# Two-bank query head, joined column units and one moved remainder in a two-block fp32 transformer kernel

## What is computed

```python
def second_block(x, norm1_g, w_in, ..., normf_g):
    h = x
    xn = rmsnorm_2(h, norm1_g)
    q_a, k_a, v_a, q_r, f_r, i_r, g_r = split(xn @ w_in)       # 7 x 512 columns
    attn = moba_attention(q_a, k_a, v_a)
    rec  = hgrn2(q_r, f_r, i_r, g_r, lb, rec_norm_g)           # f = lb + (1-lb)*sigmoid(f_r); silu(q_r); log f; cumsum
    h = h + concat([attn, rec]) @ w_out
    hn = rmsnorm_2(h, norm2_g)
    h = h + peer_2(hn, peer_wq, peer_subkeys, peer_u, peer_v)
    return rmsnorm_2(h, normf_g)

def peer_2(...):                                               # the first block has the same stage
    qp = (xb @ wq).reshape(T, HEADS, 2, 128)                   # 8 heads, two halves: 16 tiles of 128 columns
    s  = einsum('thcd,hcnd->thcn', qp, subkeys)                # 128 scores per head and half, top 16 of each
    ...                                                        # softmax over 16 experts, gelu(x u), times v
```

## Time and profile before

| | |
|---|---|
| median of 3 runs | 1984.23 us (1984.2 to 1984.7) |
| profiled execution | 1984.3 us, span 1982.5 us |
| TensorE matmul busy | 1974.8 us (100%), 13990 matmuls |
| VectorE busy | 1281.9 us (65%) |
| ScalarE busy | 1042.3 us (53%) |
| GpSimd busy | 1429.7 us (72%) |
| DMA | 177 GB/s over the span, 53.2% of 16 engines' span |

### The profile page before, as it was taken

The page is one execution under the profiler, slowest core; times in us unless marked ns, Lnnn a source line. Parts: engine busy times, 40 slices in busy tenths (PEclk is TensorE's granted clock), DMA queues, the critical chain, the costliest instruction groups (busy, mean ns, idle before and its releaser), DMA issues.

```text
span 1982.5 us, 39083 instructions
## 1 busy us (share of the span) xinstructions
PE 1974.8 (100%) x13990; PEld 1766.6 (89%) x13990; DVE 1281.9 (65%) x2178; ACT 1042.3 (53%) x1361; POOL 1429.7 (72%) x606
## 2 busy tenths in 40 slices
PE   9999999999999999999999999999999999999998
PEld 9899898888888888888889899888888888888887
DVE  5256387864766899953336738886467789994333
ACT  6556545565555544445447665556555554444444
POOL 6667878888777878854448757888877787884442
PEclk9999999999999999999999999999999999999999
DMA  8444545555555555566655345555555555555653
GB/s 273 161 139 149 179 161 186 188 183 190 177 170 175 174 169 171 177 208 206 195 186 178 123 144 166 192 187 186 182 176 172 172 178 169 175 174 181 201 190 127
DMA packets 100467, 351.44 MB, mean 177 GB/s; under 512 B 12464, under 2 KB 15408, under 8 KB 100272
## 3 DMA queue, kind: packets, MB, share of 16 engines
q1 hardware_dynamic: 99680, 348.61, 53.2%
q10 hardware_dynamic: 720, 1.92, 0.3%
HBM read 349.44 MB, written 1.05 MB: 177 GB/s over the span
## 4 chain that ended last, share of the span: by engine, by line
PE 99%; DMA 0%; DVE 0%; ACT 0%; POOL 0%; SPq 0%; issue 0%
PE ps L1259 24%; PE ps L1325 12%; PE ps L1260 12%; PE ps L1327 12%; PE ps L1328 6%; PE ps L1326 6%; PE ps L732 4%; PE ps L734 4%; PE ps L733 4%; PE ps L889 4%; PE ps L1251 3%; PE ps L891 2%; PE ps L816 1%; PE ps L1235 1%; PE ps L1137 1%; PE ps L926 1%
## 5 line engine op out<-in xcount | busy, mean ns | idle before, releaser
L653 POOL TENSOR_TENSOR wlo<-ring,whi 128x1024 fp32r<-128x1024 f32 x567 | 1375.2, 2431 | 511.3 <-ACT whi L1677 425.8
L1677 ACT ACTIVATE whi<-ring 128x1024 fp32r<-128x1024 f32 x536 | 566.5, 1060 | 718.2 <-PE ps L1328 387.2
L1259 PE MATMUL ps<-hboth,whi 128*128 128x512 f32 x2048 | 714.6, 395 | 0.0
L1260 PE MATMUL ps<-hboth,wlo 128*128 128x256 f32 x2048 | 567.7, 277 | 0.0
L1259 PEld LDWEIGHTS ps<-hboth,whi 128*128 128x128 f32 x2048 | 384.1, 188 | 87.2
L1325 PE MATMUL ps<-whi,shi 128*128 128x512 f32 x1024 | 404.2, 395 | 0.0
L1327 PE MATMUL ps<-wlo,shi 128*128 128x512 f32 x1024 | 400.4, 391 | 0.0
L1260 PEld LDWEIGHTS ps<-hboth,wlo 128*128 128x128 f32 x2048 | 384.7, 188 | 0.0
L1328 PE MATMUL ps<-whi,slo 128*128 128x256 f32 x1024 | 286.7, 280 | 0.0
L1326 PE MATMUL ps<-whi,slo 128*128 128x256 f32 x1024 | 285.7, 279 | 0.0
L1327 PEld LDWEIGHTS ps<-wlo,shi 128*128 128x128 f32 x1024 | 192.2, 188 | 43.4
(11 more groups left out here) (332 smaller groups left out, 2905.2 us busy)
## 6 DMA issues: line engine op xcount, KB each, us to landing
ring<-in_weights SPq DMA_DIRECT2D x651, 512.0 KB, 3.3
act<-in_const SPq DMA_DIRECT2D x11, 198.0 KB, 4.0
act<-in_const SPq DMA_DIRECT2D x8, 192.0 KB, 4.5
xres<-in_x SPq DMA_DIRECT2D x4, 256.0 KB, 4.9
act<-in_keys ACTq DMA_DIRECT2D x1, 1024.0 KB, 4.7
ring<-in_weights SPq DMA_DIRECT2D x2, 256.0 KB, 4.8
act<-in_fgain ACTq DMA_DIRECT2D x1, 512.0 KB, 3.4
out<-act SPq DMA_DIRECT2D x1, 512.0 KB, 2.6
```

Source lines behind the costliest of these rows:

```text
L653: pool.tensor_tensor(wlo[:, j, :], ring[:, j, :], whi[:, j, :].bitcast(F32), ALU.subtract)\
L1259: pe.matmul(bank(b), whi[:, j, c], hboth[:, :, kc, :], start=kc == 0, stop=False, skip_group_check=True)
L1260: mm = pe.matmul(bank(b, 0, S), wlo[:, j, c], hhi[:, kc, :], start=False, stop=kc == KC - 1, skip_group_check=True)
L1677: eng.activation(whi[:, j, :], ring[:, j, :], ACT.Copy).then_inc(hi_ready[j], 1)
```

## The change

Four edits are made. Units 1, 2 and 3 of the second attention go through `joined_columns()` with banks 6/7, 4/5 and 6/7; ScalarE copies the high-by-low half out of both banks to `col_part`, VectorE adds it back into the banks, and then makes the multiplication by R from there. With it the high copies of ScalarE move: one is now made ahead of the copy, one ahead of the logarithm. For the last query head of each expert stage, tile 0 goes to bank 5 and tile 1 to bank 4, each is copied by itself, and TensorE waits for the copy of head 6 before tile 1. The remainder of the third query slot of each stage goes from GpSimd to VectorE, behind the second square.

```diff
+JOINED2_BANK = {1: 6, 2: 4, 3: 6}
...
+        col_part = carve(cat_at, 2, S)[0]
...
-                lows(at, first, range(RING))
+                query = FIRST[f"q{b}"] // RING
+                lows(at, query, range(RING))
+                lows(query, query + 1, (0, 1, 3))
+                lows(query + 1, first, range(RING))
...
+                        elif i in JOINED2_BANK:
+                            joined_columns(FIRST["in2"] + HALVES * i, JOINED2_BANK[i], None if i == 1 else [(col_copied, i - 1)] * TT)
...
+                            if h + c == HEADS:
+                                pe.wait_ge(n["q_copied"], h)
+                            dst = bank(5 - c, 0, S) if h == HEADS - 1 else bank(4 + h % 2, c * S, (c + 1) * S)
+                            tile((2 * h + c) % RING, dst, R, range(4 if h + c == 1 else 0, KC))
...
+                            if i in JOINED2_BANK:
+                                highs_to(FIRST["in2"] + HALVES * i + 1 + RING)
+                                eng.wait_ge(slot_used, FIRST["in2"] + HALVES * (i + 1))
+                                if i > 1:
+                                    eng.wait_ge(col_joined, i - 1)
+                                b = JOINED2_BANK[i]
+                                eng.activation(col_part, ps[:, b:b + 2, S:2 * S], ACT.Copy).then_inc(col_parted, 1)
...
                     elif what == "rec_prep":
+                        highs_to(FIRST["in2"] + HALVES * 2 + 1 + RING)
                         eng.wait_ge(fr_bound, REC_H)
...
+                            for c in range(2):
+                                eng.wait_ge(slot_used, first_q + 2 * h + c + 1)
+                                last = eng.activation(qT[:, h % 2, c, :], bank(5 - c, 0, S), ACT.Copy)
+                            last.then_inc(n["q_copied"], 1)
...
                 square(k, 1)
+                eng.wait_ge(hi_ready[2], FIRST[f"q{i + 1}"] // RING + 1)
+                eng.tensor_tensor(wlo[:, 2, :], ring[:, 2, :], whi[:, 2, :].bitcast(F32), ALU.subtract).then_inc(lo_ready[2], 1)
                 raw_low(k, 2, rlo, rhi)
...
+                        if i in JOINED2_BANK:
+                            b = JOINED2_BANK[i]
+                            product = ps[:, b:b + 2, 0:S]
+                            eng.wait_ge(col_parted, i)
+                            eng.tensor_tensor(product, product, col_part, ALU.add).then_inc(col_joined, 1)
+                            eng.wait_ge(col_joined, i)
+                        else:
+                            product = bank(4 + i % 2).rearrange("p (j t) -> p j t", j=2)
+                            eng.wait_ge(slot_used, FIRST["in2"] + HALVES * (i + 1))
+                        eng.tensor_tensor(colT[name][:, off // P:off // P + 2, :], product, R, ALU.mult).then_inc(col_copied, 1)
```

More of the change, by code:

```diff
@@ L445, in block_program @@
         col_copied = sem("columns_copied")
+        col_parted = sem("columns_low_part_copied")
+        col_joined = sem("columns_parts_joined")
         fr_open = sem("forget_opened")
@@ L918, in joined_columns @@
                     for t in range(TT):
-                        if half == 0:
+                        if half == 0 and free is not None:
                             pe.wait_ge(*free[t])
@@ L1221, in experts @@
                                 pe.wait_ge(n["q_copied"], h - 1)
-                            tile((2 * h + c) % RING, bank(4 + h % 2, c * S, (c + 1) * S), R, range(4 if h + c == 1 else 0, KC))
+                            if h + c == HEADS:
+                                pe.wait_ge(n["q_copied"], h)
+                            dst = bank(5 - c, 0, S) if h == HEADS - 1 else bank(4 + h % 2, c * S, (c + 1) * S)
+                            tile((2 * h + c) % RING, dst, R, range(4 if h + c == 1 else 0, KC))
                             if h + c == 1:
@@ L1446, in highs_to @@
                     eng.activation(whi[:, m % RING, :], ring[:, m % RING, :], ACT.Copy).then_inc(hi_ready[m % RING], 1)
-                split[0] = end
+                split[0] = max(split[0], end)
             def turned(k):
@@ L1685, in experts @@
                     if h < HEADS:
-                        eng.wait_ge(slot_used, first_q + 2 * h + 2)
+                        if h < HEADS - 1:
+                            eng.wait_ge(slot_used, first_q + 2 * h + 2)
                         if h >= 2:
                             eng.wait_ge(n["s_ready"], h - 1)
-                        eng.activation(qT[:, h % 2, :, :], bank(4 + h % 2).rearrange("p (c t) -> p c t", c=2), ACT.Copy)\
-                           .then_inc(n["q_copied"], 1)
+                        if h < HEADS - 1:
+                            eng.activation(qT[:, h % 2, :, :], bank(4 + h % 2).rearrange("p (c t) -> p c t", c=2), ACT.Copy)\
+                               .then_inc(n["q_copied"], 1)
+                        else:
[3 more added lines that the diff above has]
+                            last.then_inc(n["q_copied"], 1)
                         for c in range(2):
@@ L2164, in attention2 @@
                             take_scale(2)
-                        eng.wait_ge(slot_used, FIRST["in2"] + HALVES * (i + 1))
-                        eng.tensor_tensor(colT[name][:, off // P:off // P + 2, :],
-                                          bank(4 + i % 2).rearrange("p (j t) -> p j t", j=2), R, ALU.mult).then_inc(col_copied, 1)
+                        if i in JOINED2_BANK:
[4 more added lines that the diff above has]
+                            eng.wait_ge(col_joined, i)
+                        else:
+                            product = bank(4 + i % 2).rearrange("p (j t) -> p j t", j=2)
+                            eng.wait_ge(slot_used, FIRST["in2"] + HALVES * (i + 1))
+                        eng.tensor_tensor(colT[name][:, off // P:off // P + 2, :], product, R, ALU.mult).then_inc(col_copied, 1)
                     elif what == "m_values":
```

## The result

The changed kernel takes 1988.47 us (median of 16 runs, 1988.04 to 1989.32) against 1984.45 for the kernel before (1983.86 to 1985.89): the ratio is 1.0020, with a 95% interval of 1.0013 to 1.0027. It is 4.0 us slower, where 1.05 us of gain were forecast and 1985.4 was the upper end of the range. The profiled execution took 1988.04 us, with a span of 1986.2.

What follows compares the result with a forecast made beforehand. TensorE was taken to bound the kernel, with matmuls covering 1974.8 of 1982.5 us. Savings of 0.33 + 0.58 + 0.14 - 0 = 1.05 us off 1984.3 gave 1983.2 us, with a range of 1982.4 to 1985.4.

Steps and rivals of the forecast that it cites:

- the part on the last query head: End of each stage's queries: an earlier last copy removes TensorE's 0.07 us of standing, 0.14 us in two blocks, at no cost.
- The sum: Whole kernel: 0.33 + 0.58 + 0.14 - 0 = 1.05 us off the profiled execution's 1984.3 us, giving 1983.2 us.
- the cadence among the rivals: Expert stage: changed arrival flips 1024 pairs from 0.346 to 0.353 us, costing 7 us, near 1990; chance 0.02.
- The joined units: Units 1 to 3 of the second attention: 5.65 in place of 5.76 us each, 0.33 us saved for three.
- the other cadence: Joined units of the second attention run at 0.346 us a pair: 0.66 us saved in all, 1982.9 us; chance 0.11.
- the nearest row: Joined units: the first attention's cadence, 0.353 us a pair, was taken because pairs there also directly follow matmuls of 256 columns.
- The moved remainder: Third query tile of each stage: subtraction on VectorE ends TensorE's standing and slow restart, 0.30 + 0.28 = 0.58 us saved.
- What gets later: VectorE in the second attention: running sum 2.3 to 3.0 us late, 0.1 after level 2's factor, no cost to TensorE.
- The running sum: VectorE in the second attention: once shifted, it finds GpSimd at the end of a remainder, after lasting 4.35 us before.
- The slack: Turn of the second attention's first probabilities: 0.80 us before, 0.47 us when TensorE is 0.33 us early.
- the late chain: Second attention: delayed levels make TensorE wait at the first turn; 2.3 us late costs 1.8 us, 1985.0 us; chance 0.22.

Runs made afterwards that it cites:

- the single edit: The kernel before with the last query head's edit alone (two banks, two copies): 1989.64 us against 1984.26, ratio 1.0026.
- the kernels with 16 and with 17 fillers: The changed kernel with its 16 short matmuls (29 ns each) on iota ahead of each expert stage's first pair, and with 17: 1988.47 and 1983.10 us.
- 17, 1 and 18 fillers: The changed kernel with 17, 1 or 18 in place of 16 short matmuls ahead of each stage's first pair: 1983.10, 1982.00 and 1983.19 us.
- 0, 15 and 16: The changed kernel with 0 or 15 short matmuls ahead of each stage's first pair, and with its own 16: 1987.43, 1992.33 and 1988.47 us.
- the one whose copies both wait: The changed kernel, but ScalarE waits for both tiles of the last query head ahead of the first copy: 1983.40 us, ratio 0.9998.
- the kernel before with 14: The kernel before with 14 in place of 16 short matmuls ahead of each stage's first pair: 1984.18 us, ratio 1.0001.

## Why the prediction was wrong

The step that failed is in the part on the last query head: "the 0.07 us goes, in two blocks 0.14 us ... Cost: nothing". The mechanism was as told and the 0.07 us did go, twice. But that standing lay eight scores and 16 short matmuls (1.4 us) ahead of a row of 416 equal pairs, and with it taken away and nothing else changed the row ran in the slower of its two cadences. The sum had no term for a cost outside the edited place. The cost is 5.5 us (the single edit, its gain counted in: +5.4 in the medians), some forty times the gain.

I had the cadence among the rivals, with a chance of 0.02, and put it at near 1990. What I set against it was wrong: "both stages start behind the same instructions as before". They do, and it is no argument: the kernels with 16 and with 17 fillers start behind the same instructions too. My own had the same form at 353 and at 346 ns a pair in one kernel; that should have told me that the cadence isn't fixed by the instruction, and that an edit ahead of such a row can put the whole row at stake, here 2.75 us a stage. As for size, I took one stage of 1024 pairs at 7 ns; it was two stages with 416 each at 6.6. That 1990 came near 1988.47 is in part luck: the two errors, in the number of stages and of pairs, work against each other.

The other steps, one by one:

- The joined units. Forecast 0.33 us, with 0.66 in the other cadence; measured 0.64. From 1052.97 to 1069.69 are 16.72 us, of which 0.08 is the start behind the transposes, for 48 pairs: 346.7 ns each. The choice of the nearest row ("pairs follow directly on matmuls of 256 columns") failed: the first unit follows on the two transposes of the token scale. Whether that is why they ran fast isn't shown; one short matmul ahead of the units of the first attention left those slow. The Trainium skill (TensorE: Matmul & The Clock Gate, section Back-to-back issue gap) gives a formula for the gap of a single warm matmul, by which a pair takes an estimated 325 ns. The rows here have two values, 346.7 and 353.3, and neither is that.
- The moved remainder. Forecast 0.30 and 0.28, measured 0.29 and 0.28. The subtraction started at 245.53 and took the 1.22 us of the earlier trace rows, and the distances of the third tile are 0.12 us from its first matmul on, as said. One reading was off without effect: from 248.43 and 248.65 in the earlier trace rows, and 0.12 us for each distance behind them, the third tile's half ended near 249.97, and with the standing gone at 249.67, not at 249.7 and 249.6.
- What gets later. Forecast: the running sum 2.3 to 3.0 us late, 0.1 at the end. The stretch lies 1.87 us later on the clock as a whole (TensorE at the token scale: 1050.96 before, 1052.83 after). The second factor of level 2 on VectorE before, then, after, GpSimd's remainder, the running sum beside it and the same factor:

```profile
1083.12 1.77 DVE L2220 TENSOR_TENSOR act<-act 128x512 f32<-128x512 f32 x1
```

```profile
1067.48 2.42 POOL L657 TENSOR_TENSOR wlo<-ring,whi 128x1024 fp32r<-128x1024 f32 x1 [1.07 <-ACT whi L1458]
...
1067.84 4.21 DVE L2225 TENSOR_TENSOR_SCAN act<-act 128x1024 f32<-128x1024 f32 x1
...
1085.27 0.69 DVE L2256 TENSOR_TENSOR act<-act 128x512 f32<-128x512 f32 x1
```

Against 1063.50 the sum is 4.34 - 1.87 = 2.5 us late; the factor starts 2.15 - 1.87 = 0.3 late, lasts 0.69 us in place of 1.77, and so ends 0.8 early, where 0.1 late was forecast. Shorter waits for GpSimd gave the lateness back, as said, but not piece by piece as followed. The running sum was to meet GpSimd at the end of a remainder; it met it 0.36 us into one, and lasted nearly as long as before. In both kernels the sum ends 2.15 us after that remainder does (1065.71 before, 1069.90 after). The relief came in the factors behind it. ScalarE and TensorE at the first turn, against the earlier trace rows (the last line is cut off by the window, at two of six transposes):

```profile
1099.00 1.48 ACT L1646 ACTIVATE act<-act,stat 128x128 f32<-128x128 f32 x4
...
1100.82 0.38 PE L1128 MATMUL ps<-ident,act 128*128 128x128 f32 x2
```

The slack fell from 0.80 to 0.34 us (0.47 were forecast with TensorE 0.33 us early; it was 0.64), and TensorE did not stand. The strongest rival, the late chain at 0.22, did not come.

So the four parts came in mechanism as told, the joined units with twice the forecast gain, and the range was missed because of what followed the last query head. What stays open is what in the start decides. The evidence leaves no rule: by its times a kernel has the same cadence in nearly all its executions, it differs with 29 ns of filler, and it is neither odd against even nor late against early. A phase isn't excluded, nor shown. Take the fillers' time modulo 120 ns, the distance of the query tiles' matmuls, as an estimate: 17, 1 and 18 fillers then lie at 13, 29 and 42 ns and are fast, 0, 15 and 16 at 0, 75 and 104 and are slow. With the standing counted in, the kernel before and the one whose copies both wait lie near 50 and are fast, as that would have it; but the kernel before with 14 lies at 109 and was fast too. Whether weight loads, the reading of the moving data or the banks' writes lock into step can't be seen in a trace that has starts and modelled ends only.

## What to carry to other kernels

When a long row of equal matmuls is the kernel, read its distance between starts before and after every edit that touches anything ahead of it, however small the edit; the busy share, the chain and the waits all look the same. If the distance has changed, put one short instruction ahead of the row, or one more or less, and measure again, before you judge the edit that you made. Here that turned the rows of both stages, and did not turn that of the first attention. And where one form shows two distances in a trace, price the change between them over the whole row as a case of its own.

## What the hardware showed that I had not expected

- One pair (512 and 256 columns) has two stable distances, 346.7 and 353.3 ns, at the same granted clock of 1.00. Single distances repeat in the first with a period of two pairs (233, 117, 231 and 112 ns between starts), in the second with a period of three (233, 117, 241, 120, 236 and 113). In some kernels the joined units of the second attention repeat with a period of one pair (230 and 117 ns), at the same mean of 346.7. Each cadence was held for all 416 pairs of the stretch, and in one kernel the slow one for a stage of 1024.
- 29 ns of useless work ahead of each of two stages took 5.4 us off the program, and with 0.19 us of standing in each the stages were 2.75 us shorter.
